# Streaming encoder layer with product-key experts: the sample tokens move from the first to the last group of tiles, and their expert rows fill 128 partitions

## The chip, the cores and the metric

The kernel runs on one core of a Trainium2 chip, in float32. The metric is the device time of one execution in microseconds (us). Five engines work side by side, each through its own list of instructions in order: TensorE (PE), VectorE (DVE), ScalarE (ACT), GpSimd (POOL) and SyncE (SP, which here only issues DMAs). They wait for each other through semaphores. SP and POOL issue nearly all DMAs; POOL's are gathers of expert rows, addressed by an index per partition.

## What is computed

One layer over 1024 prompt tokens and 64 sample tokens. Everything up to `h` is called the mix here; the last line is the expert part.

```
xn = rmsnorm(x)
z  = xn @ w_in                       # 1024 x 5632: q k v | f i q g | gate_a gate_b
o_a = band attention (own chunk of 64 + 8 chunks before it, learned bias over distance)
o_b = HGRN2 recurrence in chunks of 64, 4 heads, state 128 x 128
h  = x + (sigmoid(gate_a) * (o_a @ w_a) + sigmoid(gate_b) * (o_b @ w_b)) @ w_out
# experts: 8 heads; in each, top 16 of 128 x 128 product keys; per token and chosen expert e:
y  = h + sum over 8 heads x 16 e of gate_e * gelu(xn2 . u_tab[e]) * v_tab[e]
```

`u_tab` and `v_tab` have 16384 rows of 1024 floats, so a token reads 8 x 16 rows of 4 KB from each. The sample tokens attend to a cache of 512 keys and values and start from a given state; the prompt starts from zero.

## The kernel before

**Tiles and groups.** Tokens are cut into eight prompt tiles of 128 rows (0 to 7) and the sample tile (`SAMPLE`, 64 rows). `GROUPS` orders them in five groups: sample and 0, then 1 and 2, 3 and 4, 5 and 6, and 7 alone. The mix runs a group at a time, in stages A to I: A norm and transposes, B projections q k v, C attention, D and G gates and branch products, E projections of the recurrence, F the recurrence, H `w_out` and the second norm, I the queries and the search for the top 16 keys ("key search"). Each group streams all weights once through `wring`, a ring of three slots of 1 MB, loaded by SP in the order of use. Most stage buffers lie over each other in one array, `arena`, so a stage is entered only when ACT and DVE have left the one before (`mark_a`, `mark_d`).

**Experts.** A "head" below is one of the 8 expert heads of one tile. A head takes 16 gathers of u rows and 16 of v rows, each one DMA that puts one row of 4 KB into every partition that has a token: 128 in a prompt tile, 64 in the sample tile. They go into `ring`, 13 slots. Each u row is multiplied with the token and summed by DVE (L1549). Half of the v rows are scaled and added by DVE (L1559), the other half by TensorE, as a product with a diagonal matrix that ACT makes of the weights (L854, `diag`). The v rows of a head follow two heads after its u rows.

**What sets the order.** `interleave` writes out, at build time and for every engine alike, the heads in order and between their items the steps of the mix. The rest of group g's key search and then the mix of group g+1 are spread evenly, by costs in `slices`, over the heads of group g. So no engine chooses; a late row or a late step holds what is queued behind it. The mix of group 0 and its first key search stand in front of all heads, the heads of the last group behind all mixes (with its own key search between them, 2.5 times as dense as even spacing).

**Start.** SP first loads small constants, the sub keys, the sample's state and the tokens. The bias by distance is one line of 767 numbers per attention head in 8 partitions; L427 expands it, each of 128 rows shifted by one, into `rel_scr` in DRAM (2560 KB), and stage C reads two pieces of it per head. The transposed sub keys go to DRAM too (L430), and ACT's stage B of group 0 waits for that.

## Time and profile before

| | us |
|---|---|
| median of 3 runs (range) | 4497.34 (4483.53 to 4503.79) |
| the profiled execution, its own time | 4459.93 |
| its span in the trace | 4458.2 |
| first gather issued | 441.55 |
| busy: PE, DVE, ACT, POOL | 3141.0, 3094.0, 843.8, 2651.6 |
| moved by DMA | 1408.39 MB, of it gathers 1149.91 MB |

The span is the length of the traced execution, and the device time lies 1.7 us above it. Busy times are sums over the span and engines overlap, so none of them is a bound by itself. PEclk is the clock that TensorE was granted, as a share of full speed. The DMA share is the mean busy share of 16 DMA engines. A row of the windows gives in this order: the stretch, its length, the busy time (and instructions) of PE, of PE's weight loads, of DVE, ACT and POOL, then PEclk, the DMA share and GB/s.

### The profile page before, as it was taken

To read this page: it belongs to the slowest core of one execution; us is meant where nothing else is said; L and a number is where in the kernel's file an instruction comes from. 1 tells how busy PE (TensorE), PEld (TensorE's weight loads), DVE (VectorE), ACT (ScalarE), POOL (GpSimd) and SP (SyncE) were. 2 spreads that over 40 slices of the span, in tenths; PEclk is the share of its full clock that TensorE was granted. 3 is DMA by queue.
4 is the path that set the end of the run, shared out by engine and by line. 5 is a ranking of instruction groups with operands and counts; after the bars stand their busy time and mean duration, and the time that the engine had idled before them with its cause. 6 is when DMAs were issued, how large, how long until landed. Compare 5 with 4: busy or idle time off the path is not lost. (4 is left out here: it accounts for less than half of the span.)

```text
span 4458.2 us, 36425 instructions
## 1 busy us (share of the span) xinstructions
PE 3141.0 (70%) x11064; PEld 1982.6 (44%) x11064; DVE 3094.0 (69%) x6491; ACT 843.8 (19%) x2079; POOL 2651.6 (59%) x2349
## 2 busy tenths in 40 slices
PE   3968558997777468876875588868765667666556
PEld 3847314464454235653652265636532345343212
DVE  0142996648849986579579956595699764858975
ACT  1221112222111123122111222211111121111101
POOL 0000566647747676568456766585577765766776
PEclk9778658598898678987987698988887788788777
DMA  5415758999999899999999999999999999999999
GB/s 130 128 59 168 179 158 198 236 287 343 355 345 356 318 340 343 396 348 346 355 346 333 332 330 385 358 349 364 334 393 346 372 374 380 359 384 372 369 404 363
DMA packets 531664, 1408.39 MB, mean 316 GB/s; under 512 B 47952, under 2 KB 223568, under 8 KB 530704
## 3 DMA queue, kind: packets, MB, share of 16 engines
q0 software_dynamic: 317856, 1149.91, 71.4%
q1 hardware_dynamic: 211088, 246.98, 17.2%
q10 hardware_dynamic: 2528, 9.18, 0.6%
q8 instruction: 91, 1.49, 0.1%
q14 instruction: 101, 0.83, 0.1%
HBM read 1385.98 MB, written 19.92 MB: 315 GB/s over the span
## 5 line engine op out<-in xcount | busy, mean ns | idle before, releaser
L854 PE MATMUL PS<-ring,diag 128*128 128x512 f32 (+1 forms) x2304 | 1481.5, 783 | 828.9 <-DMA ring<-in_peer_v,idx 590.0
L558 POOL DMA_INDIRECT ring<-in_peer_u,idx x1152 | 1347.0, 1169 | 730.1 <-issue 313.2
L558 POOL DMA_INDIRECT ring<-in_peer_v,idx x1152 | 1286.4, 1117 | 632.5 <-DVE hid L1549 316.0
L1549 DVE CUSTOM_DVE_ANT_0 ring<-ring,xt 128x1024 f32<-128x1024 f32 (+1 forms) x1152 | 1396.7, 1220 | 357.3 <-DMA ring<-in_peer_u,idx 218.5
L854 PEld LDWEIGHTS PS<-ring,diag 128*128 128x128 f32 (+1 forms) x2304 | 488.1, 230 | 1541.2 <-issue 1197.7
L574 PE MATMUL PS<-xnT,wring 128*128 128x256 f32 (+2 forms) x3840 | 781.4, 365 | 164.8 <-DMA wring<-in_w_in 94.8
L574 PEld LDWEIGHTS PS<-xnT,wring 128*128 128x128 f32 x3840 | 695.7, 204 | 287.7 <-issue 156.8
L1559 DVE SCALAR_TENSOR_TENSOR acc<-ring,wk,acc 128x1024 f32<-128x1024 f32 (+1 forms) x576 | 739.5, 1284 | 62.0 <-DMA ring<-in_peer_v,idx 49.0
L544 POOL DMA_DIRECT2D xt<-xn_scr x9 | 5.4, 602 | 423.9 <-DMA xn_scr<-arena 423.9
L1170 ACT ACTIVATE diag<-ident,wk 128x128 f32<-128x128 f32 (+1 forms) x576 | 203.3, 387 | 229.1 <-PE PS L854 135.4
L578 PE MATMUL PS<-wring,xnT 128*128 128x256 f32 (+1 forms) x864 | 201.7, 392 | 21.9 <-DMA wring<-in_w_in 21.8
L578 PEld LDWEIGHTS PS<-wring,xnT 128*128 128x128 f32 (+1 forms) x864 | 162.7, 190 | 66.3 <-DMA wring<-in_w_in 27.2
L1297 DVE SCALAR_TENSOR_TENSOR arena<-PS,bias 128x640 f32<-128x640 f32 (+3 forms) x72 | 47.9, 665 | 190.3 <-DMA bias<-rel_scr 90.3
L578 PE MATMUL PS<-wring,arena 128*128 128x256 f32 (+1 forms) x576 | 143.4, 410 | 41.1 <-DVE arena L1445 34.3
L578 PEld LDWEIGHTS PS<-wring,arena 128*128 128x128 f32 (+1 forms) x576 | 114.7, 201 | 74.4 <-issue 49.3
L574 PE MATMUL PS<-arena,wring 128*128 128x256 f32 (+2 forms) x640 | 126.5, 352 | 3.9 <-DMA wring<-in_w_branch_b 2.5
L1141 ACT ACTIVATE arena<-PS 128x256 f32<-128x256 f32 (+1 forms) x72 | 27.6, 383 | 521.5 <-PE PS L822 353.1
L574 PEld LDWEIGHTS PS<-arena,wring 128*128 128x128 f32 x640 | 110.1, 192 | 27.2 <-issue 11.3
L1242 DVE TENSOR_TENSOR arena<-PS,arena 128x256 f32<-128x256 f32 (+2 forms) x40 | 15.3, 383 | 147.0 <-PE PS L574 146.9
L1155 ACT ACTIVATE arena<-arena 128x16 f32<-128x16 f32 (+1 forms) x72 | 22.2, 308 | 495.8 <-DVE arena L1506 495.5
L662 PEld LDWEIGHTS PS<-kT,arena 64*128 64x128 f32 (+1 forms) x560 | 83.3, 214 | 44.4 <-issue 35.6
L662 PE MATMUL PS<-kT,arena 64*128 64x128 f32 (+2 forms) x560 | 99.2, 328 | 3.9 <-ACT mark_a L865 2.6
(170 smaller groups left out, 2686.6 us busy)
## 6 DMA issues: line engine op xcount, KB each, us to landing
wring<-in_w_in SPq DMA_DIRECT2D x110, 1024.0 KB, 16.4
wring<-in_peer_query SPq DMA_DIRECT2D x40, 1024.0 KB, 11.7
wring<-in_w_out SPq DMA_DIRECT2D x20, 1024.0 KB, 10.3
ring<-in_peer_u,idx POOLq DMA_INDIRECT x1152, 7.1
ring<-in_peer_v,idx POOLq DMA_INDIRECT x1152, 7.0
bias<-rel_scr SPq DMA_DIRECT2D x80, 144.0 KB, 6.1
wring<-in_w_branch_a SPq DMA_DIRECT2D x10, 1024.0 KB, 23.8
wring<-in_w_branch_b SPq DMA_DIRECT2D x10, 1024.0 KB, 14.7
```

Source lines behind the costliest of these rows:

```text
L558: pool.indirect_dma_start(ring[0:tile_rows[tn], n % R, :], None, u_tab if kind == "u" else v_tab, bass.IndirectOffsetOnAxis(ap=idx[0:tile_ ...
L574: mm = pe.matmul(PS[:, n % 2, 0:W], w[:, k, s * P:(s + 1) * P], act_in[:, k, 0:W], start=(k == 0), stop=(k == nk - 1))
L578: mm = pe.matmul(PS[0:rows, n % 2, 0:ncol], act_in[:, k, c0:c0 + rows], w[:, k, :], start=(k == 0), stop=(k == nk - 1))
L662: mm = pe.matmul(PS[0:rows, bank + n // 4, (n % 4) * P:(n % 4) * P + nk], q, kk[p0:p0 + 64, h // 2, 0:nk], start=True, stop=True)
L854: mm = pe.matmul(PS[0:rows, 6 + half, :], diag[0:rows, seq % ND, 0:rows], ring[0:rows, n % R, 512 * half:512 * (half + 1)], start=(h == 0 ...
L1141: act.activation(s1[0:rows, o % 2], PS[0:rows, 2 + o % 2, 0:2 * P] .rearrange("p (a b) -> p a b", a=2), ACT.Copy).then_inc(tk_cp, 1)
L1155: act.activation(ge[0:rows, :], cv[0:rows, :], ACT.Exp, bias=ncv[0:rows, :], accum_out=gsum[0:rows, :]).then_inc(tk_exp, 1)
L1170: act.activation(diag[0:rows, seq % ND, 0:rows], ident[0:rows, 0:rows], ACT.Copy, scale=wk[0:rows, q % 2, k:k + 1]).then_inc(diag_made, 1)
L1242: dve.tensor_tensor(M[:, c, 0:W], PS[:, n % 2, 0:W], sg[:, c, 0:W], ALU.mult)\
L1297: dve.scalar_tensor_tensor(out=sc[0:rows, i % 2, 0:w], in0=flat[0:rows, 0:w], scalar=SCALE, in1=bias[0:rows, bh % 2, off:off + w], op0=ALU ...
L1549: dve.tensor_tensor_reduce(row, row, xt[0:rows, s, :], 1.0, 0.0, ALU.mult, ALU.add, hid[0:rows, m % 2, k:k + 1]).then_inc(dve_used, 1)
L1559: dve.scalar_tensor_tensor(out=acc[0:rows, s, :], in0=ring[0:rows, n % R, :], scalar=wk[0:rows, q % 2, k:k + 1], in1=acc[0:rows, s, :], op ...
```

## The change

The groups become: tile 0 alone, 1 and 2, 3 and 4, 5 and 6, and last the sample with tile 7. So group 0 is 128 tokens wide instead of 192, and the last group 192 instead of 128.

The sample's expert part goes to 128 partitions: partitions 0 to 63 take head h and partitions 64 to 127 head h + 4 of the same 64 tokens. The tile then has 4 double heads (`heads_in`), and there are 68 heads in all instead of 72. `xt` is loaded twice, the upper half of `acc` is cleared, and the two halves are added at the end by two products on TensorE (`folded`); `sel` is a matrix that adds the halves in TensorE's v rows. The key search of the sample is done on 128 partitions as well.

The bias line goes to DRAM (`rel_line`) and is expanded from there to `rel_scr` by a DMA from DRAM to DRAM. The small loads and the sub keys go from SP's queue to ACT's. `bias` and `gain_hgrn` move into `arena`, and the cache gets its own buffers there (`kC`, `vC`); that makes room for `kS` and `vS` and for a ring of 14 slots. Two pieces of bias are loaded ahead of stage C, and `gain_hgrn` once per group. Each stage A clears the two corners of `bias` again.

```diff
-GROUPS = [[(SAMPLE, 64, 0), (0, 128, 64)], [(1, 128, 0), (2, 128, 128)], [(3, 128, 0), (4, 128, 128)],
-          [(5, 128, 0), (6, 128, 128)], [(7, 128, 0)]]
+GROUPS = [[(0, 128, 0)], [(1, 128, 0), (2, 128, 128)], [(3, 128, 0), (4, 128, 128)],
+          [(5, 128, 0), (6, 128, 128)], [(SAMPLE, 64, 0), (7, 128, 64)]]
...
-R = 13
+R = 14
...
+def heads_in(tid):
+
+    return PH // 2 if tid == SAMPLE else PH
...
# SP
-            sp.wait_ge(relE, 1)
-            lines = rel[:, 0:767]
-            sp.dma_start(rel_scr, bass.AP(lines.tensor, lines.offset + 127, [list(lines.ap[0]), [-1, P], [1, WIN]]))\
-              .then_inc(rel_out, 16)
-            sp.wait_ge(sk_cp, 4)
-            sp.dma_start(sk_scr, skTs.rearrange("p a b -> p (a b)")).then_inc(sk_out, 16)
...
+                    sp.wait_ge(rel_mid, 16)
+                    sp.dma_start(rel_scr, bass.AP(rel_line.tensor, 127, [[768, HA], [-1, P], [1, WIN]]))\
+                      .then_inc(rel_out, 16)
...
# POOL
+                if tid == SAMPLE:
+                    pool.dma_start(xt[DEC:P, tn % 2, :], xn_scr[tid * P:tid * P + rows, :]).then_inc(xt_in[tn % 2], 16)
+                    pool.memset(acc[DEC:P, tn % 2, :], 0.0).then_inc(acc_clear, 1)
...
                 pool.indirect_dma_start(
-                    ring[0:tile_rows[tn], n % R, :], None, u_tab if kind == "u" else v_tab,
-                    bass.IndirectOffsetOnAxis(ap=idx[0:tile_rows[tn], at:at + 1], axis=0)).then_inc(row_in[n % R], 16)
+                    ring[:, n % R, :], None, u_tab if kind == "u" else v_tab,
+                    bass.IndirectOffsetOnAxis(ap=idx[:, at:at + 1], axis=0)).then_inc(row_in[n % R], 16)
...
# TensorE
+                if kind == "S" and m == stn:
...
+                        mm = pe.matmul(PS[0:DEC, 6 + half, :], ident[:, DEC:P], acc[:, m % 2, 512 * half:512 * (half + 1)],
+                                       start=False, stop=True, skip_group_check=True)
+                    mm.then_inc(folded, 1)
...
# ACT
+            act.wait_ge(relE, 1)
+            act.dma_start(rel_line[:, 0:767], rel[:, 0:767]).then_inc(rel_mid, 16)
...
+            act.wait_ge(sk_cp, 4)
+            act.dma_start(sk_scr, skTs.rearrange("p a b -> p (a b)")).then_inc(sk_out, 16)
```

The start of SP's list, before (`arena<-in_x_*` are the tokens, `wring` the first weights, `arena<-in_cache_attn_k` and `v` the cache):

```order
L424 DMA arena<-in_x_sample 64x1024
L424 DMA arena<-in_x_prompt 128x1024
L427 DMA rel_scr<-arena 1024x1x640 [waits relE]
L430 DMA sk_scr<-T 128x2048 [waits sk_cp]
L436 DMA wring<-in_w_in 128x8x256 x3
L436 DMA wring<-in_w_in 128x8x256 [waits pj_ready] x3
L456 DMA arena<-in_cache_attn_k 128x4x512 [waits bar_dve,bar_act]
L457 DMA v<-in_cache_attn_v 128x4x512
```

And after the change, from the first instruction on (`arena<-rel_scr` are the bias pieces):

```order
L448 DMA arena<-in_x_prompt 128x1024
L454 DMA wring<-in_w_in 128x8x256 x3
L485 DMA rel_scr<-rel_line 1024x1x640 [waits rel_mid]
L454 DMA wring<-in_w_in 128x8x256 [waits pj_ready] x3
L470 DMA arena<-rel_scr 64x576 [waits rel_out]
L470 DMA arena<-rel_scr 64x576 x3
```

The first three weight blocks now stand ahead of the expansion of the bias instead of behind it, and two heads' bias is asked for ahead of stage C.

TensorE's list in the attention of tiles 1 and 2 (group 1's stage C), before; `ring,diag` are v rows of the heads of group 0, here the sample's, the other rows the scores, transposes and values of one attention step after another:

```order
L854 MATMUL PS<-ring,diag 64x512 x2
L673 MATMUL PS<-ident,arena 128x128 x2
L854 MATMUL PS<-ring,diag 64x512 x2
L662 MATMUL PS<-kT,arena 128x128 x2
L673 MATMUL PS<-ident,arena 128x128 x3
L686 MATMUL PS<-v,arena 128x64 x2
L854 MATMUL PS<-ring,diag 64x512 x2
L662 MATMUL PS<-kT,arena 128x128 x3
L673 MATMUL PS<-ident,arena 128x128 x2
L686 MATMUL PS<-v,arena 128x64 x3
L854 MATMUL PS<-ring,diag 64x512 x2
```

The same place after the change, where the heads are tile 0's:

```order
L898 MATMUL PS<-ring,diag 128x512 x2
L705 MATMUL PS<-masks,arena 128x128 x2
L718 MATMUL PS<-v,arena 128x64 x3
L694 MATMUL PS<-kT,arena 128x128 x2
L705 MATMUL PS<-masks,arena 128x128 x3
L718 MATMUL PS<-v,arena 128x64 x2
L898 MATMUL PS<-ring,diag 128x512 x2
L694 MATMUL PS<-kT,arena 128x128 x3
L705 MATMUL PS<-masks,arena 128x128 x2
L718 MATMUL PS<-v,arena 128x64 x3
L694 MATMUL PS<-kT,arena 128x128 x2
L898 MATMUL PS<-ring,diag 128x512 x2
```

About twice as many rows of the mix stand between two v rows, since group 1's whole mix is spread over 8 heads and no longer over 16. In groups 1, 2 and 3 the density is as before.

## Rows read from the trace of the kernel before

**Rows 1.** Page: the span

```profile
span 4458.2 us, 36425 instructions
```

**Rows 2.** Windows, columns as told above: group 0's B, C, D, E, F twice, G, H

```profile
73.00:115.00 42.00, 40.43 (x217) 35.60 (x218) 0.00 (x0) 7.02 (x22) 0.00 (x0) 1.00 0.46 156
115.00:168.00 53.00, 44.84 (x227) 36.18 (x224) 17.73 (x49) 19.74 (x69) 0.00 (x0) 0.53 0.36 109
168.00:207.00 39.00, 37.76 (x220) 36.82 (x220) 2.87 (x9) 6.21 (x17) 0.00 (x0) 0.90 0.41 135
207.00:258.00 51.00, 48.82 (x251) 39.80 (x249) 5.55 (x14) 10.48 (x21) 0.00 (x0) 1.00 0.38 124
258.00:290.00 32.00, 16.25 (x84) 11.07 (x84) 15.57 (x40) 7.62 (x21) 0.00 (x0) 0.50 0.12 33
290.00:340.00 50.00, 22.91 (x107) 17.98 (x108) 28.65 (x46) 9.79 (x22) 0.00 (x0) 0.60 0.14 48
340.00:375.00 35.00, 34.10 (x199) 33.54 (x198) 5.74 (x17) 4.72 (x12) 0.00 (x0) 0.95 0.57 184
375.00:418.00 43.00, 33.42 (x142) 23.36 (x141) 6.08 (x13) 5.73 (x11) 0.00 (x0) 0.89 0.47 150
```

**Rows 3.** Windows: the experts' phases, from the first gather to the end

```profile
442.00:985.00 543.00, 406.98 (x1141) 223.13 (x1141) 403.86 (x997) 96.14 (x269) 328.91 (x303) 0.66 0.83 209
985.00:1461.00 476.00, 360.65 (x1284) 239.87 (x1283) 357.48 (x720) 90.84 (x212) 306.84 (x259) 0.86 0.95 349
1461.00:2380.00 919.00, 674.06 (x2404) 439.66 (x2404) 689.76 (x1440) 188.17 (x451) 598.87 (x517) 0.84 0.95 350
2380.00:3293.00 913.00, 673.57 (x2440) 438.60 (x2440) 680.36 (x1386) 190.13 (x447) 594.00 (x513) 0.84 0.95 349
3293.00:4148.00 855.00, 546.74 (x1960) 324.35 (x1960) 642.62 (x1345) 152.84 (x370) 588.37 (x513) 0.79 1.00 370
4148.00:4458.00 310.00, 173.72 (x262) 57.91 (x260) 225.56 (x370) 37.02 (x94) 225.24 (x219) 0.77 0.98 381
```

**Rows 4.** Timeline, POOL and DVE: first gather; first and last of nine tile ends

```profile
441.55 0.94 POOL L558 DMA_INDIRECT ring<-in_peer_u,idx  x1 [14.81 <-DVE gates L1523]
...
984.48 1.28 DVE L1569 TENSOR_TENSOR acc<-PS,acc 64x512 f32<-64x512 f32 x2 [1.03 <-PE PS L854]
...
4447.36 1.29 DVE L1569 TENSOR_TENSOR acc<-PS,acc 128x512 f32<-128x512 f32 x2 [2.05 <-PE PS L854]
```

**Rows 5.** Groups by form, DVE and PE: expert rows at 128 and 64 partitions

```profile
L1549 DVE CUSTOM_DVE_ANT_0 ring<-ring,xt 128x1024 f32<-128x1024 f32 x1024 | 1242.1, 1221 | 324.1 <-DMA ring<-in_peer_u,idx 207.6 <-DMA arena<-in_x_prompt 65.3 <-ACT mark_a L865 50.1
L1559 DVE SCALAR_TENSOR_TENSOR acc<-ring,wk,acc 128x1024 f32<-128x1024 f32 x512 | 658.0, 1285 | 59.1 <-DMA ring<-in_peer_v,idx 46.1 <-issue 10.4
L1549 DVE CUSTOM_DVE_ANT_0 ring<-ring,xt 64x1024 f32<-64x1024 f32 x128 | 154.6, 1210 | 33.2 <-ACT mark_a L865 22.0 <-DMA ring<-in_peer_u,idx 11.0
```

**Rows 6.** Windows: ten us while the bias is expanded

```profile
40.00:50.00 10.00, 0.00 (x0) 0.00 (x0) 0.00 (x0) 0.00 (x0) 0.00 (x0) 1.00 0.49 58
```

**Rows 7.** DMA issues: engine, operation, count, KB each, us from issue to landing

```profile
sk_scr<-T SPq DMA_DIRECT2D x1, 1024.0 KB, 51.3
```

**Rows 8.** Timeline, PE: products 192, 128 and 256 columns wide

```profile
367.87 5.36 PE L574 MATMUL PS<-arena,wring 128*128 128x192 f32 x32
...
3934.78 3.84 PE L574 MATMUL PS<-xnT,wring 128*128 128x128 f32 x32 [1.84 <-DMA wring<-in_w_in]
...
96.04 14.57 PE L578 MATMUL PS<-wring,xnT 128*64 128x256 f32 x64
```

**Rows 9.** Timeline, DVE: ends of the first and the sixth key search

```profile
441.05 0.23 DVE L1523 TENSOR_SCALAR gates<-arena 64x16 f32<-64x16 f32 x1
...
517.52 0.23 DVE L1523 TENSOR_SCALAR gates<-arena 64x16 f32<-64x16 f32 x1
```

**Rows 10.** Chain of waits, longest first: who waited for whom

```profile
POOL ring L558 <- DVE hid L1549: 335.9, 132, 22.0
...
POOL ring L558 <- PE PS L854: 298.3, 124, 13.7
```

More of the change, by code:

```diff
@@ L67, in slices @@
     nt = len(GROUPS[g])
+    nh = sum(heads_in(t[0]) for t in GROUPS[g])
     a = [6.0, 2.5, 0.5, 1.5, 0.5, 3.0] + [2.0] * nt
@@ L92, in units @@
             now.append(("G", uq, 0, 0))
-        if vq is not None and vq % PH == PH - 1:
-            now.append(("S", vq // PH, 0, 0))
-            ended[vq // PH] = m
+        if vq is not None and last_head(vq):
+            now.append(("S", HEAD[vq][0], 0, 0))
+            ended[HEAD[vq][0]] = m
         for tn, last in ended.items():
@@ L131, in interleave @@
             costs += [(steps, c) for c in slices(g + 1)[0][:slices(g + 1)[1]]]
-        last = m + len(GROUPS[g]) * PH
+        last = m + sum(heads_in(t[0]) for t in GROUPS[g])
         items = [it for now in work[m:last] for it in now]
@@ L194, in plan_projections @@
             add(g, "H", "w_out", 8, 256 * i, 256, "tm", "o")
-        for i in range(8):
-            add(g, "I", "w_query", 8, 256 * i, 256, "fm", "query")
+        half = heads_in(GROUPS[g][0][0])
+        for i in range(half):
+            for h in range(i, PH, half):
+                add(g, "I", "w_query", 8, 256 * h, 256, "fm", "query")
     return blocks, products
@@ L224, in build @@
         for ti in range(len(GROUPS[g])):
-            for h in range(PH):
+            for h in range(heads_in(GROUPS[g][ti][0])):
                 top_no[g, ti, h] = len(top_no)
@@ L639, in mix @@
                 enter(pe, g, "C")
-                if g == 0:
+                if g == SG:
                     pe.wait_ge(vc_in, 16)
@@ L810, in mix @@
                 qn = by_stage[g, "I"]
+                turns = [(ti, h) for ti in range(nt) for h in range(heads_in(tiles[ti][0]))]
+                first = heads_in(tiles[0][0])
+                each = len(qn) // first
                 def key_scores(i):
-                    ti, h = divmod(i, PH)
+                    ti, h = turns[i]
                     if ti == 0:
-                        for n in qn[2 * h:2 * h + 2]:
+                        for n in qn[each * h:each * (h + 1)][-2:]:
                             pe.wait_ge(pj_free[n % 2], n // 2 + 1)
@@ L1125, in mix @@
                 qn = by_stage[g, "I"]
+                turns = [(ti, h) for ti in range(nt) for h in range(heads_in(tiles[ti][0]))]
+                each = len(qn) // heads_in(tiles[0][0])
                 def copy_scores(i):
-                    ti, h = divmod(i, PH)
-                    rows = tiles[ti][1]
+                    ti, h = turns[i]
                     if ti == 0:
@@ L1327, in mix @@
                 enter(dve, g, "D")
+                if g == SG:
+                    dve.wait_ge(kv_out, 32 * sum(len(k_tiles[q]) for q in range(g + 1)))
                 yield
```

287 lines of the change are left out of this document (160 added, 127 removed).

## The prediction, made before the changed kernel was run

> **What bounds the kernel now.** I read the windows first, cut at the ends of stages and tiles. They show three regimes, which sum to the span [rows 1].
>
> The first is the start. Until 441.55 us no expert row is asked for [rows 4], so all of group 0's mix and one key search lie bare. TensorE works 38 to 49 us of each projection stage but stands idle for half of stage F, where it and DVE wait for each other [rows 2]. Ahead of stage B there is a hole to 73 us: TensorE's first weights come late. While the bias is expanded the DMAs move 58 GB/s at a share of 0.49, so half the DMA engines are fully busy at very little [rows 6], and the first weights and the sub keys' store stand behind that in the queue [rows 7].
>
> The second is the steady state, from 985 to 4148 us: sixteen full heads take 919, 913 and 855 us [rows 3]. The DMA share is 0.95 to 1.00 at 349 to 370 GB/s, and DVE and TensorE are busy 64 to 76%. Here the DMAs bind, and only fewer bytes or fewer gathers would help.
>
> The third lies between, 442 to 985 us, with the sample's eight heads. It moves only 209 GB/s, yet takes 543 us [rows 3]. A row on 64 partitions costs DVE 1210 ns and on 128 partitions 1221 ns [rows 5]: DVE pays by the elements of one partition, so half of its work there is wasted, and so is a slot and a gather of POOL's. The sample's eight heads take 543 us, with two heads' u rows ahead of them, and tile 0's eight full heads only 476, for nearly twice the bytes. This regime and the start are what the change touches.
>
> **The change part by part.**
>
> *Start.* Stage lengths shrink with the width of the group. A pass of 32 records took 5.36 us at 192 columns and 3.84 us at 128, so 0.168 and 0.12 us each, and 64 records over 256 columns 14.57 us, or 0.228 us each [rows 8]. Stage by stage, with the length of before from [rows 2]:
> - B: 128 records at 0.12 and 32 at 0.228 give 22.7, with ends 24 (was 42).
> - C: one tile with one block of keys instead of two tiles. I take 26 (was 53): half of the steps are gone, and the short ones stay. Bounds 17 and 53, as no row shows a tile alone there.
> - D: 192 records at 0.12 give 23, with the transposes 28 (39). G: 24 (35).
> - E: 128 at 0.12 and 64 at 0.228 give 30, with ends 32 (51).
> - F: the sample's 32 us go, tile 0's 50 stay.
> - H: 64 records at 0.228 are 14.6, and the waits for tokens, norm and transposes 11: 26 (43).
> - First key search: 23.5 before (418 to 441.55), 22 now.
>
> These sum to 232. The hole before B: the weights now stand ahead of the expansion, as the lists show. What remains is ACT's wait for the sub keys' store, which took 51.3 us behind the expansion [rows 7]. ACT got there at about 19 us, so with a clear queue it would be done near 30, and as slow as before at 70. I take 36. The expansion itself: stage B's 4 to 5 MB go beside it, and it is needed only at 60. It moves 2.6 MB. At a full share the projections' DMAs give 124/0.38 = 326 GB/s [rows 2], so all engines would need 8 us; at the 50 to 58 GB/s of [rows 6] it needs 52 us, from about 14 to 66. I take half the engines at that full rate, 16 us; even the slow end delays stage C by only 6 us, though it would also hold up the store. The first gather then comes at 36 + 232 = **268 us** (before 441.55), bounds 255 and 310.
>
> The Trainium skill, "DMA: Bandwidth & Descriptors", section "Why a DMA increments its semaphore by 16 and not by 1", says that the number of DMA engines used is the largest up to 16 that divides the slowest dimension of both sides, which is 8 here before and after. It speaks against this edit: coming from DRAM does not spread the copy. The share of 0.49 agrees, and the rule does not say why those eight were slow. If only their number mattered, the copy would take 52 us again, which is the slow end above.
>
> *Phase 0*, tile 0's heads with all of the mix of tiles 1 and 2. Before, this stretch plus the sample's heads took 543 + 476 = 1019 us. Two ways to size it:
> - From DMA-bound phases. With no mix beside it, a gather costs (4447 - 4148)/219 = 1.37 us [rows 3, 4]. Sixteen heads are 512 gathers, 701 us, so a pair's mix adds 919 - 701 = 218. Phase 0 has 288 gathers (8 heads of u and v, and the u rows of two heads more): 395 + 218 = 613.
> - From what it replaces. Eight sample heads leave, each 16 u rows at 1.22 us, their read-outs and 8 v rows at 1.285, about 31 us of DVE, together 248; and eight key searches, which stood 15.3 us apart [rows 9] with some 3 us of rows in each, so 96. 1019 - 248 - 96 = 675.
>
> I take the middle, **645 us**. Check: the mix of a pair takes TensorE 674 less sixteen heads. A head takes 173.7/8 = 21.7 [rows 3], so 327 of mix, and phase 0 would load it 327 + 174 = 501, or 78%. DVE: (690 - 16 x 31) - 96 + 9 x 31 = 377, or 58%. Both are near what the steady phases show, so it can be done, but with little to spare on TensorE. At twice the density a v row waits behind twice the mix.
>
> *Phases 1 and 2*: same tiles, same order, **919 and 913**. The clearing of the bias corners and the one 256 KB load per group are hidden by the DVE's and SP's idle time.
>
> *Phase 3*, heads of 5 and 6: the mix beside them is now sample and 7 instead of 7. Between 855 (7 alone) and 913 (a pair) [rows 3]; the bytes hardly change, so I take **885**.
>
> *End*: 310 us for tile 7's heads and the tail [rows 3], and now four double heads of the sample ahead of them, 128 gathers at 1.37 = 175: **485**. Their folding and the second load of `xt` are a few us each behind rows in the ring.
>
> *Ring of 14*: POOL waited 336 + 298 us for a slot [rows 10]. If one slot more took a fourteenth of it, it would give 45. Where the DMAs bind it gives nothing. I take nothing and keep 45 for the range.
>
> Sum: 268 + 645 + 919 + 913 + 885 + 485 = 4115, against 4458.2, so 343 less. Of it 174 come from the start, 374 from phase 0, and 205 are given back behind. With the 1.7 us outside the span, 4117 against 4459.9 of the profiled execution. That execution is 37 us under the median of the runs, and I add the same: **4154, said as 4150**.
>
> A second way by bytes: some 53 MB move before 441 us [rows 2], so 1355 MB move in 4016 us after it. At the steady 350 GB/s they need 3870, and 268 + 3870 = 4138. The two agree within 23 us.
>
> **Rivals.**
> 1. *Phase 0 chokes* (chance 0.20). TensorE's list is twice as dense, and stage F is a chain between DVE, PE and ACT with expert rows between its steps. Group 0's mix bare took 345 us [rows 2] for 192 tokens, so about 440 for 256; nothing overlapped would be 440 + 9 heads of DVE at 31 + 84 for seven key searches = 803, so 158 more. With the slow expansion (35) it gives 4150 + 193 = 4340; half of it 4245. For it speaks that DVE and PE took turns in 442 to 985 us; against it that the same engines overlap well in the second row of [rows 3].
> 2. *The DMAs gain more* (0.15). Phase 0 at 613, the ring's 45, phase 3 at 860, a start at 255: 4150 - 32 - 45 - 25 - 13 = 4035. For it speak POOL's waits [rows 10], against it the shares of 0.95 and more.
> 3. *Bytes bind everywhere* (0.02). Total bytes are the same, so if the DMAs ran at one capped rate, the early start would be paid back. For 4460 they would have to average 1355/(4460 - 268) = 323 GB/s, where [rows 3] shows 349 to 381. The Trainium skill, "DMA: Bandwidth & Descriptors", section "Where 436 GB/s comes from", gives about 358 GB/s as one core's share of DRAM bandwidth. By it the end would be at 268 + 1355/0.358 = 4053 at best; 381 GB/s in the last row is above it, so the trace does not bear it out as a cap.
> 4. *Slower* (0.03). TensorE's clock falls to its lower level (1.2 of 2.4 GHz) all through phase 0. Its 501 us of work were measured at a granted clock of 0.84; at 0.5 they are 842 us. If it is then busy 75% of the time, as in 442 to 985 us (407 of 543), phase 0 lasts 1120 us, 475 more than I take, and the kernel ends at 4625. It turns slower where phase 0 passes 990 us. The first row of [rows 3] has a clock of 0.66, lower than the others; but there TensorE waited for DVE's key searches, of which half go.
>
> **How the numbers follow.** My forecast has 0.60: 4100 to 4210, from phase 0 between its bounds, the start's 255 to 310 and phase 3's two ends. Rival 2 reaches to 4035 and rival 1 to 4340; leaving out the outer part of each gives 4050 to 4285. A change of 0.5% is about what this kernel's measurement can tell. Faster holds the forecast and rivals 1 and 2, 0.95; rival 3 is no change, 0.02; rival 4 slower, 0.03.
>
> **What would show it.** The first gather at 255 to 310 us, and TensorE's first projection by 40. Tile 0's end at 268 + 645 = 913 us. Phases 1 and 2 within 10 us of before at a share of 0.95. 2176 gathers instead of 2304, all on 128 partitions, and about 119 us less of DVE (64 u rows at 1.22 and 32 v rows at 1.285). The end 485 us long. I am wrong if phase 0 passes 750 us, if the steady phases move by more than 2%, or if the sub keys' store still lands near 70 us.

## The result and the profile after

The changed kernel takes 4318.29 us (median of 4 runs, 4306.14 to 4325.2), the kernel before 4500.24 (4 runs). The ratio is 0.960 with a 95% interval of 0.9566 to 0.9634: 182 us less, a little over half of the 343 that I predicted. 4318 lies above my range. Of the four executions of e8_costs_sample_first, told below, one took 5808.7 us and its median leaves that one out.

The page of the changed kernel, span and busy times, against [rows 1] and the table:

```profile
span 4321.0 us, 35603 instructions
...
PE 2999.9 (69%) x10940; PEld 1929.3 (45%) x10940; DVE 2950.6 (68%) x6193; ACT 819.4 (19%) x2020; POOL 2567.2 (59%) x2221
```

DVE has 143 us less to do and PE 141. The gathers are 2 x 1088 now. Next the windows of the changed kernel: the start up to the first gather, then the phases as in [rows 3] (tile 0; tiles 1 and 2; 3 and 4; 5 and 6; the sample's four double heads; tile 7 and the tail), columns as there.

```profile
0.00:255.00 255.00, 173.62 (x1102) 157.88 (x1103) 58.66 (x167) 56.30 (x146) 8.63 (x27) 0.83 0.61 196
...
255.00:971.00 716.00, 523.40 (x2124) 386.70 (x2122) 473.21 (x1101) 144.24 (x368) 341.73 (x301) 0.84 0.84 293
971.00:1895.00 924.00, 667.09 (x2404) 435.28 (x2404) 688.68 (x1441) 188.37 (x451) 599.70 (x519) 0.84 0.95 349
1895.00:2830.00 935.00, 686.66 (x2448) 449.58 (x2448) 690.92 (x1439) 190.51 (x452) 592.07 (x515) 0.83 0.94 344
2830.00:3779.00 949.00, 662.87 (x2456) 415.47 (x2456) 663.22 (x1374) 184.12 (x458) 638.16 (x515) 0.79 0.93 336
3779.00:3988.00 209.00, 104.12 (x152) 25.27 (x152) 170.61 (x403) 24.55 (x66) 146.15 (x131) 0.64 0.89 331
3988.00:4321.00 333.00, 182.11 (x256) 59.07 (x256) 205.34 (x274) 31.26 (x79) 240.73 (x217) 0.73 0.93 352
```

Read it against the sum that I predicted:

| term | predicted | measured | difference |
|---|---|---|---|
| first gather | 268 | 255 | -13 |
| phase 0 | 645 | 716 | +71 |
| phase 1 | 919 | 924 | +5 |
| phase 2 | 913 | 935 | +22 |
| phase 3 | 885 | 949 | +64 |
| sample's double heads | 175 | 209 | +34 |
| tile 7 and tail | 310 | 333 | +23 |
| sum | 4115 | 4321 | +206 |

The start came out better than forecast, and all behind it worse. One more thing is read from the table: phases whose work the change does not touch (phase 2, tile 7) are longer as well. That asks for a second profile of the kernel before.

Phase 0 in four pieces: key search, A, B and the first half of C; the rest of C, D and E; F to H; stage I with the first search of group 1:

```profile
253.00:450.00 197.00, 113.51 (x528) 92.49 (x528) 133.84 (x397) 40.69 (x118) 85.74 (x78) 0.75 0.76 259
450.00:600.00 150.00, 142.78 (x611) 112.48 (x612) 68.06 (x117) 36.21 (x90) 66.69 (x58) 0.95 0.93 333
600.00:840.00 240.00, 172.88 (x685) 120.97 (x684) 155.00 (x247) 44.37 (x99) 105.48 (x90) 0.85 0.78 263
840.00:971.00 131.00, 96.23 (x319) 62.75 (x317) 118.18 (x347) 22.97 (x62) 83.82 (x75) 0.85 0.95 355
```

The DMAs stand idle 24% of the first piece and 22% of the third, where no engine is over 72% busy: in the first DVE has 134 of 197 us, in the third PE 173 of 240. POOL, which issues the gathers, is held by them there: 105 us in the first piece and 105 in the third it waits for a slot or for the key search. So the two are taken to wait for each other there, with rows between; this is read from the busy times and not tested alone.

### The profile page after: what moved, and what is told of

It is laid out like the page before. It is cut to its first block, busy times and chain, and to the rows that moved or that the text cites. A ratio compares the mean times of both kernels' runs of the same rounds, so it can differ in the third digit from the quotient of the medians.

```text
span 4321.0 us, 35603 instructions
## 1 busy us (share of the span) xinstructions
PE 2999.9 (69%) x10940; PEld 1929.3 (45%) x10940; DVE 2950.6 (68%) x6193; ACT 819.4 (19%) x2020; POOL 2567.2 (59%) x2221
## 3 DMA queue, kind: packets, MB, share of 16 engines
q8 instruction: 90, 1.47, 0.1%
## 4 chain that ended last, share of the span: by engine, by line
DVE 26%; PE 19%; POOL 15%; issue 10%; DMA 10%; another core or an unknown queue 3%; ACT 2%; SPq 1%; DVEq 0%; ACTq 0%; POOLq 0%
POOL ring L590 15%; PE PS L606 9%; DVE ring L1609 8%; DVE acc L1621 5%; PE PS L610 5%; DMA wring<-in_w_in 4%; PE PS L898 4%; DMA ring<-in_peer_v,idx 4%; DMA arena<-in_x_prompt 1%; DVE arena L1578 1%; DVE arena L1577 1%; DMA xn_scr<-arena 1%; DVE arena L1550 1%; DVE arena L1542 1%
## 5 line engine op out<-in xcount | busy, mean ns | idle before, releaser
L898 PE MATMUL PS<-ring,diag 128*128 128x512 f32 (+1 forms) x2176 | 1380.0, 774 | 771.6 <-DMA ring<-in_peer_v,idx 482.7
L590 POOL DMA_INDIRECT ring<-in_peer_u,idx x1088 | 1233.3, 1134 | 810.8 <-DVE hid L1609 402.8
L590 POOL DMA_INDIRECT ring<-in_peer_v,idx x1088 | 1314.6, 1208 | 649.5 <-issue 310.8
L1609 DVE CUSTOM_DVE_ANT_0 ring<-ring,xt 128x1024 f32<-128x1024 f32 x1088 | 1320.2, 1221 | 365.4 <-DMA ring<-in_peer_u,idx 200.5
L1621 DVE SCALAR_TENSOR_TENSOR acc<-ring,wk,acc 128x1024 f32<-128x1024 f32 x544 | 699.5, 1286 | 58.4 <-DMA ring<-in_peer_v,idx 40.4
L1224 ACT ACTIVATE diag<-masks,wk 128x128 f32<-128x128 f32 x512 | 186.5, 396 | 264.9 <-PE PS L898 103.4
L1354 DVE SCALAR_TENSOR_TENSOR arena<-PS,arena 128x256 f32<-128x256 f32 (+4 forms) x72 | 47.8, 664 | 156.4 <-remote 63.0
L1197 ACT ACTIVATE arena<-PS 128x256 f32<-128x256 f32 x68 | 26.2, 385 | 491.3 <-PE PS L860 202.2
L694 PE MATMUL PS<-kT,arena 64*128 64x128 f32 x480 | 82.5, 319 | 41.5 <-ACT arena L1036 19.5
L694 PEld LDWEIGHTS PS<-kT,arena 64*128 64x128 f32 x480 | 68.6, 217 | 69.4 <-issue 43.0
```

The costliest lines, as they stand in the source:

```text
L590: pool.indirect_dma_start(ring[:, n % R, :], None, u_tab if kind == "u" else v_tab, bass.IndirectOffsetOnAxis(ap=idx[:, at:at + 1], axis=0 ...
L694: mm = pe.matmul(PS[0:rows, bank + n // 4, (n % 4) * P:(n % 4) * P + nk], q, kk[p0:p0 + 64, h // 2, 0:nk], start=True, stop=True)
L898: mm = pe.matmul(PS[0:rows, 6 + half, :], diag[:, seq % ND, 0:rows], ring[:, n % R, 512 * half:512 * (half + 1)], start=(h == 0 and k == m ...
L1224: act.activation(diag[:, seq % ND, 0:rows], sel[:, :] if rows == DEC else ident, ACT.Copy, scale=wk[:, q % 2, k:k + 1]).then_inc(diag_made, 1)
L1354: dve.scalar_tensor_tensor(out=sc[0:rows, i % 2, 0:w], in0=flat[0:rows, 0:w], scalar=SCALE, in1=bias[0:rows, bh % 2, off:off + w], op0=ALU ...
L1609: dve.tensor_tensor_reduce(row, row, xt[:, s, :], 1.0, 0.0, ALU.mult, ALU.add, hid[:, m % 2, k:k + 1]).then_inc(dve_used, 1)
```

## The experiments

Theories. **A**: the time missed comes from the order, the mix between the expert rows, and from the sample's own mix. **B**: the ring's new slot or the new layout slows the gathers. **C**: idle time of the DMAs is only moved about, so it is nearly the same wherever the sample stands. **D**: a gather into 64 partitions is slow by the DMAs' way into SBUF. Ratios are to the kernel before on the same chip; that kernel's median lay between 4499 and 4519 us in the four sets, each on a chip of its own, so that ratios compare across sets better than microseconds do.

### The ring

```diff
-R = 14
+R = 13
```

> The changed kernel with 13 slots in the ring instead of 14. Theory A (the missed time comes from the order in which the mix stands between the expert rows and from the sample's own mix): 4305 to 4345 us, its end after tile 6 still some 540 us. Theory B (the 14th slot and the new layout of the buffers slow the gathers themselves): 4230 to 4290 us, the end near 485 us and the steady phases at 919 and 913 us.

Measured: 4322.5 us (4 runs), ratio 0.9583 (0.9561 to 0.9605), and from tile 6's end on 543 us (542 in the changed kernel). The 14th slot is worth nothing that can be measured, and B falls with regard to it.

### The sample's place, with double heads

```diff
-GROUPS = [[(0, 128, 0)], [(1, 128, 0), (2, 128, 128)], [(3, 128, 0), (4, 128, 128)],
-          [(5, 128, 0), (6, 128, 128)], [(SAMPLE, 64, 0), (7, 128, 64)]]
+GROUPS = [[(SAMPLE, 64, 0), (0, 128, 64)], [(1, 128, 0), (2, 128, 128)], [(3, 128, 0), (4, 128, 128)],
+          [(5, 128, 0), (6, 128, 128)], [(7, 128, 0)]]
```

> The changed kernel with the groups of before (sample and 0 first, 7 alone last), the double heads of the sample kept. Theory A: first gather at 400, the phase of 12 heads with the mix of 1 and 2 850, then 919, 913, 855 and 310 as before, 4247 in all, with the usual distance of the median 4270 to 4310 us: the move of the sample gave nothing, the double heads gave it all. Rival (my prediction's sum, by which the start's 170 us are a net gain of the move): 4400 us or more.

Measured: 4317.0 us, ratio 0.9571 (0.9534 to 0.9609). Within the noise this is the changed kernel's time. **The move of the sample is worth nothing in time**, and my sum, which had it as a net gain, is wrong there. Windows of this kernel, same columns: start; sample and tile 0; 1 and 2; 3 and 4; 5 and 6; tile 7 and tail.

```profile
0.00:416.00 416.00, 315.53 (x1646) 269.61 (x1647) 93.55 (x239) 90.17 (x243) 9.97 (x29) 0.81 0.43 133
416.00:1281.00 865.00, 601.79 (x2232) 401.92 (x2230) 617.60 (x1415) 163.74 (x420) 510.12 (x432) 0.82 0.90 321
1281.00:2198.00 917.00, 669.95 (x2404) 436.89 (x2404) 687.89 (x1437) 187.99 (x451) 592.40 (x516) 0.84 0.95 351
2198.00:3121.00 923.00, 677.78 (x2440) 446.97 (x2440) 679.54 (x1390) 188.57 (x446) 593.19 (x514) 0.84 0.95 347
3121.00:3981.00 860.00, 539.32 (x1960) 322.68 (x1960) 642.05 (x1350) 152.37 (x371) 584.99 (x516) 0.78 0.99 369
3981.00:4313.00 332.00, 182.35 (x260) 60.75 (x260) 225.32 (x367) 37.08 (x94) 236.02 (x218) 0.72 0.94 354
```

Against the changed kernel: the start is 161 us longer here, and the first phase 149 longer, with four heads more in it. All of it comes back: the phase of 5 and 6 is 89 shorter, the sample's 209 at the end are absent, and 19 lie in the two phases between. The length of each window times (1 - DMA share) is the time in which the DMAs idle. It is 237 + 87 + 46 + 46 + 9 + 20 = 445 us here; in the changed kernel 99 + 115 + 46 + 56 + 66 + 23 + 23 = 428. The earlier start takes away 138 us of idle time and 121 of it come back: 28 in phase 0, 57 beside the heads of 5 and 6, where the DMAs had been busy 99%, and the rest between and at the end. So the sum holds in two orders, as theory C has it. It is an account of where the idle time lies, and no cause: it holds where work is moved. Seen from POOL, the later start is paid for in the same way. Between its first and last gather POOL waits some 716 us here and 846 in the changed kernel, and its issues take 39 us less.

The start is also 28 us shorter here than the 444.5 of the kernel before's second profile (below), which lies in the start's own changes, and the first phase is 865 us and not 1031, for the most part what double heads are worth in this place.

### The double heads

The sample stays in the last group, as 8 heads on 64 partitions.

```diff
-    return PH // 2 if tid == SAMPLE else PH
+    return PH
...
-                    ring[:, n % R, :], None, u_tab if kind == "u" else v_tab,
-                    bass.IndirectOffsetOnAxis(ap=idx[:, at:at + 1], axis=0)).then_inc(row_in[n % R], 16)
+                    ring[0:tile_rows[tn], n % R, :], None, u_tab if kind == "u" else v_tab,
+                    bass.IndirectOffsetOnAxis(ap=idx[0:tile_rows[tn], at:at + 1], axis=0)).then_inc(row_in[n % R], 16)
```

(The folding goes too, and the key scores of the upper half.)

> The changed kernel with the sample in the last group but as 8 heads on 64 partitions, so 128 gathers more at the same bytes. If a gather costs by its bytes (DMA-bound end): 4318 plus 0 to 20 us. If eight half heads cost DVE's time, 31 us each: plus 40 to 60. If a gather of 64 rows costs as much as one of 128: plus 165 us.

Measured: 4506.4 us (10 runs), ratio 0.9976 (0.996 to 0.9992), 188 us above the changed kernel and 184 above e1_ring13 on the same chip. It is the third of my cases, a gather of 64 rows that costs as much as one of 128 (plus 165). **Without the double heads the gain is gone.** That does not make the other parts worth nothing: the start's queue alone gives some 45 us (below), and the kernel here, which has it, is 8 us faster than the kernel before. By these figures the move with single heads would cost some 37 us; that was not run alone. Here the sample's eight heads take 379 us, against 209 for four double ones:

```profile
3804.00:4183.00 379.00, 189.49 (x293) 46.51 (x292) 315.61 (x701) 40.97 (x117) 279.35 (x255) 0.69 0.83 206
```

The DMAs are 83% busy at 206 GB/s. Tile 7's gathers behind it reach 351 GB/s at 92%. So a packet into these partitions takes longer, unless something else differs. What POOL waited for in this stretch, in all, times, longest (`issue` is its own time between two gathers):

```profile
POOL ring L590 <- issue: 74.8, 237, 1.5
POOL ring L590 <- DVE hid L1602: 15.1, 9, 4.4
```

With the 279.35 us of busy time these gaps make 354 of 379 us in which POOL does nothing but issue 253 gathers; DVE held it for 15. Over the whole execution issues and gaps sum to 3373 us here and to 3201 in the changed kernel, 172 of the 197 us between the two profiles.

### Which partitions

One thing is changed against the kernel just above.

```diff
+                p0 = 32 if tile_rows[tn] == DEC else 0
...
-                    ring[0:tile_rows[tn], n % R, :], None, u_tab if kind == "u" else v_tab,
+                    ring[p0:p0 + tile_rows[tn], n % R, :], None, u_tab if kind == "u" else v_tab,
```

> e3_single_heads with one thing changed: the 64 rows of a sample gather land in partitions 32 to 95 instead of 0 to 63, same count and bytes. The sums over the sample's experts then use rows that lie beside other tokens; the work is the same. Theory D (64 rows into the lower half of the partitions can use only half of the paths that the DMAs have into SBUF, so they run at 206 GB/s): the eight half heads fall from 379 to 310 to 330 us, where DVE's 316 us of work bind, and the whole to 4440 to 4460. Rival (a gather costs the same whatever it carries, or DVE sets it): 379 and 4506 as before.

Measured: 4460.6 us, ratio 0.992 (0.9897 to 0.9943) against 0.9976.

```profile
3748.00:4118.00 370.00, 190.12 (x292) 47.13 (x292) 314.95 (x704) 41.51 (x119) 275.76 (x257) 0.68 0.70 210
...
POOL ring L591 <- issue: 78.2, 246, 2.7
POOL ring L591 <- DVE hid L1603: 9.2, 5, 3.6
```

The DMA share falls from 0.83 to 0.70 at 210 GB/s, so a transfer is quicker when it reaches both halves of the partitions. The Trainium skill, "SBUF — State Buffer", section "Door 1: The DMA port swizzle (why `[64,N]` ≈ `[32,N]`)", has it that partitions 0 to 63 are reached through 8 of 16 ports only. The trace agrees: the partitions alone change the share. But the stretch becomes only 9 us shorter, and not 50 to 70. So D names a true cost that does not set the time.

What does? DVE has 315 us of work in both, 83 and 85% of the stretch, and looks like the limit; my prediction had said so of it. But a limit holds the others up, and DVE held POOL for only 15 and 9 us. POOL was issuing for 354 us in both, 96% of the stretch here. So by these waits it is the number of gathers that sets the length, and the double heads halve it. The price of one agrees wherever no mix stands beside the heads: 1.50 us in e3_single_heads and 1.46 here with 64 rows each; 1.45, 1.45 and 1.47 with 128 rows (tile 7 in the changed kernel and in e2_sample_first, tile 0 in e11_mix_then_heads). With 128 rows the DMAs are 93 to 94% busy too, and the two limits cannot be told apart; with 64 rows in partitions 32 to 95 they can. Why an issue lasts 0.94 us mostly and up to 2.0 at times is not shown, and no run gave DVE less work at the same count.

By the ratios e10_other_partitions gains 0.56% on e3_single_heads, 25 us. The profiles differ by more, 36 us of it in the phase before, where two sample heads' u rows are gathered beside a mix (973 and 937 us), and 20 ahead of any sample row, where the two kernels do the same. The phase before took 949, 963 and 981 us in the profiles of the changed kernel, e1_ring13 and e4_bias_from_sbuf, so such differences are scatter until shown otherwise.

### The start's queue

```diff
+            sp.wait_ge(relE, 1)
+            lines = rel[:, 0:767]
+            sp.dma_start(rel_scr, bass.AP(lines.tensor, lines.offset + 127, [list(lines.ap[0]), [-1, P], [1, WIN]]))\
+              .then_inc(rel_out, 16)
...
-                    sp.wait_ge(rel_mid, 16)
-                    sp.dma_start(rel_scr, bass.AP(rel_line.tensor, 127, [[768, HA], [-1, P], [1, WIN]]))\
-                      .then_inc(rel_out, 16)
```

> The changed kernel with the bias expanded from 8 partitions of SBUF, ahead of the weights on SP's queue, as before the change. Both theories: TensorE's first projection at 70 to 75 us instead of 38, first gather 35 us later, and since nothing behind it is faster for that, 4350 us. If the DMAs bind everything behind the start the same.

Measured: 4365.4 us, ratio 0.9662 (0.9633 to 0.9692), 47 us above the changed kernel. Timeline of TensorE, the first projection, here and then in the changed kernel:

```profile
72.34 7.83 PE L606 MATMUL PS<-xnT,wring 128*128 128x128 f32 x53 [46.66 <-DMA wring<-in_w_in]
```

```profile
38.41 11.78 PE L606 MATMUL PS<-xnT,wring 128*128 128x128 f32 x84 [1.50 <-ACT mark_a L909]
```

The first gather comes at 288.7 us instead of 255.4, as expected, 33 us later, and tile 0's end 34 us later. Behind it the two profiles differ in the phase of 5 and 6 alone by more than 13 us (981 and 949), which is within its scatter. This part of the change is a clear gain: here nothing was moved to pay for it, and it is not paid back. The source of the expansion and its place in the queue were changed together, so their shares stay open.

### TensorE or DVE in phase 0

```diff
-ON_PE = frozenset(range(1, TOPK, 2))
+ON_PE = frozenset(range(1, TOPK, 4))
```

> The changed kernel with 4 of 16 v rows on TensorE instead of 8, the other 12 on DVE. If TensorE's density sets phase 0 (718 us now, TensorE busy 75%), it loses 87 us of TensorE there and falls to 640 to 680, at the cost of DVE. If the chains through DVE set it (stage F, key search), 32 more additions of 1.285 us lengthen it: 750 us or more, and the phases of 16 heads, where DVE is then busy 84%, grow too: over 4350 in all.

Measured: 4408.5 us, ratio 0.9762 (0.9727 to 0.9797). Phase 0 takes 719 us, as before (716), and the next phase 954 (924). Neither case as I put it: TensorE lost 53 us of work in phase 0 and DVE gained 36, and the length did not move. So neither engine's load alone sets phase 0. A chain through both, in the fixed order, fits that. With all the heads in view, half of the v rows on TensorE is the better of the two shares tried.

### The sample beside tile 1

```diff
+GROUPS = [[(0, 128, 0)], [(SAMPLE, 64, 0), (1, 128, 64)], [(2, 128, 0), (3, 128, 128)],
+          [(4, 128, 0), (5, 128, 128)], [(6, 128, 0), (7, 128, 128)]]
```

> The changed kernel with groups 0 | sample, 1 | 2, 3 | 4, 5 | 6, 7. Theory C (the DMAs' idle time is only moved about: some 430 to 440 us of it in the kernel before, in the changed one and with the sample first): 4300 to 4340 us again, phase 0 near 640 as its mix is narrower, the end of 16 heads without a mix 680 to 700. Rival (the sample's mix is dear where the DMAs bind, 89 us more in the phase of tiles 5 and 6, and hidden elsewhere): 4230 to 4270.

Measured: 4322.5 us, ratio 0.9584 (0.9548 to 0.962). The third order with the same time, for C: the idle time of the DMAs comes to 429 us. But phase 0 takes 742 us and not 640, with a mix of 192 tokens: the width of a group does not tell what its mix costs.

### The mix by itself

In the first of two kernels all of tile 0's key search and the mix of 1 and 2, up to the first search of group 1, stand ahead of its heads; in the second the same is done with sample and 7, ahead of the heads of 5 and 6 (`g == 3` in the edit's place of `g == 0`).

```diff
-            while at < len(costs) and spent <= total * n / len(items):
+            while at < len(costs) and (g == 0 or spent <= total * n / len(items)):
```

> The changed kernel with nothing overlapped in phase 0: all of tile 0's key search and the mix of tiles 1 and 2 stand ahead of its first expert row. It gives the length of both apart. If the mix alone is the sum of its stages scaled up (440, with seven key searches 84, 525 in all) and the 8 heads alone 350: tile 0 ends at 1130, 4470 in all, and the overlap in the changed kernel saves 160 of 875. If the mix alone takes nearly 700 it sets phase 0 by itself, and tile 0 ends at 1300 or later.

Measured: 4528.0 us, ratio 1.0085 (1.0055 to 1.0116), slower than the kernel before by 0.9%. Seven searches and the mix up to stage H; then stage I up to the first search, and tile 0's heads. The single row is POOL's first gather after the 14 that fill the ring:

```profile
254.00:721.00 467.00, 343.82 (x1570) 297.89 (x1569) 155.15 (x444) 88.04 (x233) 13.22 (x14) 0.78 0.33 108
721.00:1176.00 455.00, 253.24 (x561) 121.42 (x559) 331.90 (x654) 45.25 (x124) 324.59 (x290) 0.74 0.94 351
...
753.68 1.68 POOL L590 DMA_INDIRECT ring<-in_peer_u,idx  x1 [482.50 <-DVE hid L1609]
```

> The changed kernel with nothing overlapped in the phase of tiles 5 and 6: the key search of 5 and 6 and the mix of sample and 7 stand ahead of its 16 heads. From the last row of tile 4's heads to the entry of stage I the mix by itself: 430 to 450 us if the sample counts for its 64 rows, 480 and more if it counts for a full tile (the mix of 1 and 2 with seven key searches took 467).

Measured (one run, 4642.3 us). From the entry of stage A to that of stage I, then the rest up to tile 6's end (stage I with its first search, the last v rows of tile 4, and the 16 heads):

```profile
2850.00:3235.00 385.00, 311.67 (x1609) 268.20 (x1610) 91.92 (x196) 86.71 (x218) 0.00 (x0) 0.75 0.33 106
3235.00:4101.00 866.00, 498.53 (x884) 194.25 (x883) 584.32 (x952) 81.03 (x215) 637.72 (x575) 0.71 0.96 356
```

The pair's mix without its searches ran from 319.5 to 721 in the first kernel, 401 us. Sample and 7 take 385. So 64 + 128 tokens cost 96% of 128 + 128 here, but the two attend to unlike numbers of keys: tile 7 and the sample to five blocks each, tiles 1 and 2 to two and three. Split at the ends of stages, B and C take 118 us against 92, and the other stages 266 against 309, 86% for 75% of the tokens. The part that does not shrink shows in TensorE's groups: 192 records of products by tokens take 43.6 us against 41.8, while 512 records as wide as the group take 91.0 against 117.3. So without attention the sample's mix lies between its share of tokens and a full tile. My expectation for this run started at the row of tile 4's heads, which does not fit a mix that begins ahead of it; the entries of the stages are used instead.

The first kernel also prices phase 0. The first row is used at 752.2. From there tile 0's heads alone take 424 us, and the searches and the mix ahead of it 498, 922 in a row, and 716 in the changed kernel. So 206 of 498 are hidden, 41%. My 645 needed 277, 56%.

### The cache's keys

```diff
-                        return [(kC[:, :, t * P:(t + 1) * P], vC[:, t, :], P) for t in range(4)] + [
-                            (kS, vS, DEC)]
+                        return [(kS, vS, DEC)]
```

> The changed kernel with the sample's attention over its own 64 keys only; the 512 keys and values of the cache are left out of it (still loaded and transposed). If its five blocks of keys make the sample's mix dear: the phase of tiles 5 and 6 goes from 949 to 905 to 920 us, 4280 in all. If stage F and the products by tokens do, which cost by steps and not by rows: 940 to 950, 4310 to 4320.

Measured: 4312.1 us, ratio 0.9535 (0.9496 to 0.9574), the phase of 5 and 6 949 us. In us this is 6 below the changed kernel, by the ratio 0.5% below e1_ring13 and e6_sample_with_1 (0.958). But the phase that was to shrink to 905 to 920 us took 949, as before. So the long attention is not what makes that phase long, as far as one profile tells where the scatter is some 30 us.

### The costs of the steps

```diff
-    b = [1.7] * (8 + 2 * nt) + [2.0]
+    fm = 3.5 * width(g) / 256
+    b = [fm] * 8 + [3.6] * (2 * nt) + [2.0]
...
-    d = [1.5] + [1.3] * 16 + [0.5]
-    e = [1.7] * (8 + 4 * nt) + [0.5]
+    d = [1.5] + ([fm] * 4 + [fm / 2] * 4) * 2 + [0.5]
+    e = [fm] * 8 + [3.6] * (4 * nt) + [0.5]
...
-    gg = [1.3] * 16 + [0.5]
-    h = [1.7] * (4 * nt) + [0.5, 2.5, 0.5, 1.5, 3.0] + [1.5] * nt
+    gg = ([fm] * 4 + [fm / 2] * 4) * 2 + [0.5]
+    h = [3.6] * (4 * nt) + [0.5, 2.5, 0.5, 1.5, 3.0] + [1.5] * nt
```

> The changed kernel with the costs of the projections' steps in the interleaving set to TensorE's time for them (3.5 us for a product of 256 columns instead of 1.3 to 1.7, 3.6 for a product by tokens instead of 1.7). If phase 0 chokes because expert rows come too thinly beside the projections and too densely beside stage F (uneven spacing): phase 0 at 650 to 690 instead of 718, the phases of 16 heads 5 to 15 us shorter each, 4250 to 4290 in all. If it is the sum of the work and not its spacing: 4310 to 4330.

Measured: **4274.9 us, ratio 0.9482 (0.9452 to 0.9512)**, 43 us below the changed kernel. Phases, from tile 0 to 5 and 6:

```profile
252.00:957.00 705.00, 515.24 (x2138) 387.11 (x2136) 484.25 (x1155) 144.99 (x371) 353.30 (x304) 0.86 0.85 302
957.00:1874.00 917.00, 652.39 (x2404) 431.17 (x2404) 694.18 (x1441) 189.86 (x453) 608.12 (x516) 0.85 0.95 351
1874.00:2788.00 914.00, 662.47 (x2444) 437.26 (x2444) 691.79 (x1419) 190.14 (x452) 602.08 (x516) 0.85 0.96 352
2788.00:3725.00 937.00, 639.07 (x2452) 401.55 (x2452) 658.56 (x1340) 183.74 (x455) 648.18 (x515) 0.82 0.94 340
```

Each phase gives 7 to 21 us, and phase 0 only 11. Spacing is a small part of phase 0's excess. The idle time of the DMAs falls to 386 us in all: other than by a move, it can be lowered.

The same costs with the sample in front:

> The true costs of e7_true_costs with the groups of before (sample and 0 first, double heads). Theory C (idle time of the DMAs is conserved, wherever the sample stands): 4260 to 4290 us, as e7_true_costs at 4275. Rival (the move gives something once phase 0 is spaced well): 4300 or more.

Measured: 4289.0 us, ratio 0.9539 (0.9494 to 0.9583), at the upper end of my first case. The ratio is 0.006 above that of the kernel above, and the two half widths together make 0.005. Whether the move gives some 0.5% once the costs are right stays open.

The costs of F and of the key search raised as well:

```diff
-    f = ([2.5, 2.5, 3.0, 4.5, 2.0] + [2.3, 1.5, 1.2, 2.0] * HB + [1.0, 0.5, 2.0, 1.5]) * nt
+    f = [1.4 * c for c in ([2.5, 2.5, 3.0, 4.5, 2.0] + [2.3, 1.5, 1.2, 2.0] * HB + [1.0, 0.5, 2.0, 1.5]) * nt]
...
-    return before + [1.5] * (6 * nh), len(before) + 6
+    return before + [2.1] * (6 * nh), len(before) + 6
```

> e7_true_costs with the costs of stage F and of the key search raised by 1.4 as well, as the DMAs still stand idle 22% of the time beside them in phase 0. If spacing is still what loses time there: phase 0 10 to 20 us shorter, 4255 to 4265. If the chains of these stages are as long as that whatever stands beside them: 4275 again or slightly worse.

Measured: 4266.3 us, ratio 0.9476 (0.9436 to 0.9517), phase 0 701 us. Not to be told from the one before. These two are the fastest kernels of the study.

The corrected costs in the kernel before:

> The kernel before with the costs of e7_true_costs and nothing else. If the uneven spacing cost the same in any order: 30 to 45 us less than the kernel before, ratio 0.990 to 0.993. If it matters only where the mix stands twice as dense: 0.998 to 1.000.

Measured: 4532.5 us, ratio 1.0032 (1.0008 to 1.0056), slightly slower. So the gain of the costs belongs to the changed kernel. I expected the contrary or nothing; why it turns there was not tried.

### The kernel before once more

> The kernel before once more, for a second profile, since its first one was 40 us faster than the median of its runs. If the gathers of tile 7 alone took 299 us there because that execution moved data faster: 315 to 325 us now, as in all four runs of the changed kernel's kind so far (322 to 324), and tiles 5 and 6 870 to 890. If the change itself slows gathers: 299 again.

Measured: 4525.0 us (one run). The phases, with the sample's and tile 0's in one row:

```profile
444.00:1475.00 1031.00, 767.43 (x2428) 464.07 (x2428) 761.09 (x1718) 187.12 (x482) 636.46 (x558) 0.75 0.86 270
1475.00:2403.00 928.00, 676.97 (x2404) 440.93 (x2404) 689.03 (x1442) 188.14 (x451) 595.58 (x518) 0.84 0.95 348
2403.00:3332.00 929.00, 680.93 (x2440) 446.04 (x2440) 680.01 (x1386) 189.38 (x447) 593.32 (x516) 0.84 0.94 346
3332.00:4188.00 856.00, 549.17 (x1960) 328.12 (x1960) 640.88 (x1347) 152.40 (x371) 587.31 (x514) 0.78 1.00 368
4188.00:4523.00 335.00, 187.07 (x260) 62.29 (x260) 225.06 (x367) 36.48 (x93) 240.04 (x217) 0.70 0.94 351
```

The same kernel, 65 us longer than the profiled execution of [rows 1]: tile 7 and the tail take 335 us and not 310, a gather there 1.47 us and not 1.34, the middle phases 928 and 929. So the changed kernel's 924, 935 and 333 are no change at all. B falls altogether, and the 50 us in three terms of my sum came from a quick execution as its base. The 37 us that I added for the median had covered most of them.

## Why the prediction was wrong, step by step

- **Start**: right, and a little better. 255 us against 268, TensorE's first projection at 38.4, and e4_bias_from_sbuf shows the queue's part: 33 us of the 189 between 444.5, the first gather in the kernel before's second profile, and 255.4. By e2_sample_first all that is not the move gives 28, and the narrower group the other 161. The sub keys' store landed 8.7 us after its issue at 30.1, far from 70. My doubt about the expansion from DRAM was without effect: issued at 25.9 us, it had landed when the first piece of bias was asked for at 52.0, so in at most 26 us, and I had taken 16.
- **Phase 0**: the step that failed most, 716 against 645. I took the middle between a gather price and a subtraction. The gather price was mis-sized: tile 0's heads alone take 424 us and not 395, a gather 1.47 us and not 1.37, since that price came from the quick execution. The overlap was mis-sized more: the mix then adds 292 and not 218, as only 41% of it and its searches is hidden. My bound from above (675) was no bound: it took DVE's 31 us for a sample head and 12 for a key search, as if what leaves takes its whole time with it.
- **Phase 3**: "between 855 and 913" was wrong as a bound. I scaled the sample's mix by its tokens. By itself it costs more than that, 385 us for the group against 401 for a pair with fewer keys, and the phase lies with the pairs (949 beside 924 and 935). That the cache's keys lengthen it is not seen. The products by tokens, which move 256 columns whatever the rows are, do not shrink; how much of the phase's 64 us they make was not shown.
- **The end**: 128 gathers at 1.37 gave 175, measured 209. At 1.46, the price in the stretches without a mix, they are 187; in e15_last_mix_bare the 512 from tile 4's end to tile 6's took 743 us, 1.45 each. The rest is a wait that my sum did not have. Ahead of tile 7's first gather POOL loads `xt` and `acc`, which have two buffers each. POOL's waits in these 209 us:

```profile
POOL ring L590 <- issue: 38.4, 126, 0.3
POOL xt L573 <- DMA out<-acc: 21.4, 1, 21.4
```

  Tile 6's result had not left its buffer yet, with only the sample's four double heads between them; with eight single heads there, in e3_single_heads, no such wait stands. DVE is busy 82% here as well, but held POOL for 2 us.
- **The double heads**: a gain, 188 us by e3_single_heads in the last group, and 166 in the first by e2_sample_first against the second profile of before. I gave two reasons, DVE's wasted work and the wasted slot and gather of POOL's. The second is what counted. I then priced the leaving heads by DVE alone, and named the DMAs as what binds where no mix stands beside; there a gather costs some 1.46 us at 206 GB/s as at 352. The even greater error is in what I made of the move: I booked 174 for the start and 374 for phase 0 as gains and 205 as paid back. By e2_sample_first all the move's parts cancel to 0. The second way by bytes could not warn me. It took 350 GB/s for all that follows the start, where phase 0 runs at 293.
- **Rivals**: rival 1 (phase 0 chokes) was the nearest, 4245 to 4340 with 0.20, and 4318 lies in it. Its place was right for a third of the miss only. Rival 3 (bytes bind everywhere) had the right idea for the move and the wrong size: it is not one capped rate, but the DMAs' idle time, which comes back elsewhere. Slower (0.03) did not come: phase 0's granted clock was 0.84.
- **My own signs of being wrong**: phase 0 stayed under 750 and the store was early, but phase 2 moved by 2.4% (935 against 913), past the 2% that I had named. By the second profile of before (929) it had not moved; the base was quick.

What stays open: why phase 3 is some 20 us longer than the pairs' phases, whether DVE would bind the sample's heads if POOL did not, and why the kernel before does not gain from the corrected costs.

## What to carry to other kernels

When a bare stretch at the start is shortened by moving work to the end, write down the idle time of the resource that binds, window by window, before and after. The start's gain counts only as far as the moved work finds idle time where it lands; beside a phase with the DMAs 99% busy it finds none. Count the instructions of the engine that issues the transfers, and not only their bytes: a gather of 64 rows took POOL as long as one of 128, and DVE too takes as long for 64 rows (1210 and 1221 ns), so filling all 128 partitions was the largest gain. A busy share does not name the limit. DVE was busy 83 to 85% and held POOL up for 9 to 15 us of 370 and more; look for who waits for an engine. Where a tile becomes short, check whether its neighbours' buffers come free in time. And profile the base twice before building a sum on its phases: here two executions differed by 1.5%. Phases repeat worse than whole times: the phase of tiles 5 and 6 took 949 to 981 us in three profiles.

## What the runs showed of the hardware

- 64 rows gathered into partitions 0 to 63 ran at 206 GB/s with the DMAs 83% busy, into partitions 32 to 95 at 210 GB/s with 70%. Same bytes and count, so the partitions alone make a transfer longer or shorter.
- Where little else held POOL, a gather cost it 1.45 to 1.50 us from one issue to the next, with 64 rows or 128, at a DMA share of 0.70 to 0.96. In one execution of the kernel before it was 1.34. Most issues last 0.94 us, some up to 2.0, and 0.30 lie between two.
- A line of 3 KB in each of 8 partitions, expanded to 2560 KB by reads that overlap, ran at 58 GB/s with a DMA share of 0.49 [rows 6], and in e4_bias_from_sbuf TensorE waited 46.66 us for the weights behind it in the queue. The same expansion from DRAM was done in at most 26 us, so at 100 GB/s or more. The Trainium skill's section on the port swizzle, named above, puts partitions 0 to 7 behind two of the 16 ports; by that rule it was the way out of SBUF that held the transfer back, and the trace agrees in so far as the copy from DRAM, with the same outer dimension of 8, ran at nearly twice the rate or more.
